# Eighteen chunks of two feed-forward down-projections in seven block products instead of eight

## The reference

```
f = jnp.square(jax.nn.relu(h @ w_ff1[l])) @ w_ff2[l]       # first block: 2048 -> 8192 -> 2048
x = x + gt2 * _rmsnorm(f, g_post_ffn[l])
...
u = jnp.square(jax.nn.relu(h @ w_up[layer]))               # second block, same sizes
x = x + _rmsnorm_2(u @ w_down[layer], norm_mlp_post[layer])
```

## Time and profile before

| | us |
|---|---|
| median of 3 runs | 2550.8 (2550.72 to 2552.91) |
| the profiled execution, its own time | 2552.28 |
| its span, first to last instruction | 2550.5 |
| TensorE matmul busy | 2518.8 (99%) |
| VectorE busy | 1743.5 (68%) |
| ScalarE busy | 1201.3 (47%) |

### The profile page before, as it was taken

One profiled execution on the slowest core, in us unless ns is written; L12 is line 12 of the kernel. 1 busy time (PEld: TensorE's weight loads), 2 busy tenths in 40 slices (PEclk: granted clock), 3 DMA queues, 4 the chain that ended last, 5 costly groups with the idle time before them and its releaser, 6 DMA issues.

```text
span 2550.5 us, 30392 instructions
## 1 busy us (share of the span) xinstructions
PE 2518.8 (99%) x12284; PEld 2102.3 (82%) x12284; DVE 1743.5 (68%) x2351; ACT 1201.3 (47%) x1740; POOL 6.4 (0%) x16
## 2 busy tenths in 40 slices
PE   7999999999999999999999999999999999999998
PEld 4887888888878888888888888888788888888887
DVE  7987988788987866556556565656765574664665
ACT  4444354533456434444344466455554443443443
POOL 0000000000000000000000000000000000000000
PEclk9999999999999999999999999999999999999999
DMA  9984376588876775555555545533545555555553
GB/s 401 415 326 166 123 278 258 196 337 334 340 297 243 283 283 193 199 187 185 200 187 195 207 158 187 192 140 144 200 176 200 182 187 205 185 198 188 183 199 142
DMA packets 78747, 567.12 MB, mean 222 GB/s; under 512 B 8800, under 2 KB 8928, under 8 KB 10256
## 3 DMA queue, kind: packets, MB, share of 16 engines
q1 hardware_dynamic: 77472, 558.09, 59.2%
q0 software_dynamic: 1136, 7.10, 0.7%
HBM read 563.06 MB, written 2.10 MB: 222 GB/s over the span
## 4 chain that ended last, share of the span: by engine, by line
PE 90%; DVE 5%; DMA 2%; ACT 2%; issue 1%; SPq 0%; DVEq 0%; ACTq 0%
PE ps L1238 20%; PE ps L1241 20%; PE ps L1239 20%; PE ps L1296 15%; PE ps L1307 8%; DMA raw<-stream_in 2%; DVE wl L2054 2%; DVE ACC L2088 1%; PE ps L1223 1%; PE ps L1329 1%; PE ps L1578 1%; ACT wh L1645 1%; PE ps L1548 1%; PE ps L1399 0%; PE ps L1333 0%
## 5 line engine op out<-in xcount | busy, mean ns | idle before, releaser
L2054 DVE TENSOR_TENSOR wl<-raw,wh 128x1024 fp32r<-128x1024 f32 x836 | 985.6, 1220 | 538.9 <-ACT wh L1645 537.9
L1645 ACT ACTIVATE wh<-raw 128x1024 fp32r<-128x1024 f32 x836 | 837.4, 1049 | 713.6 <-PE ps L1241 569.8
L1238 PE MATMUL ps<-wh,U 128*128 128x512 f32 x1344 | 525.7, 391 | 0.1
L1241 PE MATMUL ps<-wl,U 128*128 128x512 f32 x1344 | 523.8, 390 | 1.1 <-DVE wl L2054 1.1
L1239 PE MATMUL ps<-wh,U 128*128 128x512 f32 x1344 | 523.0, 389 | 0.0
L1296 PE MATMUL ps<-HT,wh 128*128 128x512 f32 x1792 | 431.7, 391 | 0.0
L1238 PE MATMUL ps<-wh,HT 128*128 128x512 f32 x1080 | 430.0, 398 | 1.0 <-DVE HT L2179 0.9
L1241 PE MATMUL ps<-wl,HT 128*128 128x512 f32 x1080 | 422.0, 391 | 1.5 <-DVE wl L2054 1.5
L1239 PE MATMUL ps<-wh,HT 128*128 128x512 f32 x1080 | 420.8, 390 | 0.0
L1296 PEld LDWEIGHTS ps<-HT,wh 128*128 128x128 f32 x1792 | 328.7, 188 | 63.8 <-issue 0.4
L1241 PEld LDWEIGHTS ps<-wl,U 128*128 128x128 f32 x1344 | 252.3, 188 | 56.4 <-DVE wl L2054 3.5
(11 more groups left out here) (306 smaller groups left out, 1499.8 us busy)
## 6 DMA issues: line engine op xcount, KB each, us to landing
raw<-stream_in SPq DMA_DIRECT2D x524, 1024.0 KB, 4.8
M<-rows_in POOLq DMA_DIRECT2D x6, 1024.0 KB, 5.0
M<-stream_in SPq DMA_DIRECT2D x3, 1024.0 KB, 10.9
y_out<-X SPq DMA_DIRECT2D x3, 512.0 KB, 2.6
X<-x_in SPq DMA_DIRECT2D x1, 1024.0 KB, 5.2
X<-x_in SPq DMA_DIRECT2D x2, 512.0 KB, 14.7
raw<-stream_in SPq DMA_DIRECT2D x1, 640.0 KB, 4.1
raw<-stream_in SPq DMA_DIRECT2D x1, 512.0 KB, 3.3
```

The costliest lines, as they stand in the source:

```text
L1238: e.matmul(o, ah, H[:, c:c + bw], start=k == k0, stop=False)
L1241: ins = e.matmul(o, ah, L[:, c:c + bw], start=False, stop=end)
L1645: e.activation(H, raw[place[n][0]][:, c:c + w], ACT.Copy).then_inc(*hi.tick(p))
L2054: e.tensor_tensor(L, raw[place[n][0]][:, c:c + w], H.bitcast(F32), ALU.subtract).then_inc(*lo.tick(p))
```

## The change

In ten down slabs, 18 chunks (`SEVEN`) are multiplied as 2 by 2 blocks, where rows `t` and steps `k` make the blocks of the hidden matrix, and steps `k` and column blocks `b` those of the weights. Seven block products are formed from sums of blocks. Three products (one from unchanged blocks, one from both, one from a sum) go straight into banks 0, 1 and 2; four go into banks 4 to 7 and are summed over the two such chunks of the slab.

- `blocksums` (VectorE): four sums of 128x512 of the raw weight blocks, into `SUMS` in `M`.
- The chunk is split in four pieces: 1024, 512, 1024 and 1024 columns; the first two come from `raw`, the last two from `SUMS`. They take four places of the ring.
- `combine` (a side task in the second up slab): four operations make the sums of the hidden blocks of both chunks at once, and one copy and one subtraction their halves. For this the hidden tiles of these chunks are kept (`KEPT`).
- `sevenout`: after the last such chunk of a slab one copy by ScalarE and eight operations of 128x512 by VectorE bring banks 4 to 7 into `y`, spread over the next two chunks (one, in the last group's second slab).
- The high half of a tile is an item of its own, `tilehigh`. It stands behind the splits of the next chunk, ahead of `tilelow`.
- `raw` is given back after the second piece's low half.

```diff
+SEVEN = {"fd20": (1, 3), "fd21": (1, 3), "fd30": (1, 3), "fd31": (1,), "gd10": (1, 3), "gd11": (1, 3),
+         "gd20": (1, 3), "gd21": (1, 3), "gd30": (1, 3), "gd31": (1,)}
...
+        if by_seven(name, i) and j == 0:
+            add("blocksums", n)
         add(*only, "split", len(pieces))
+        if by_seven(name, i):
+            pieces.append({"n": n, "ks": None, "width": 512, "w": 512 if j == 1 else 1024, "c": None, "slot": slot,
+                           "before": before, "last": j == 3, "part": j})
+            return
...
             while tiles:
+                add("tilehigh", *tiles[0])
                 add("tilelow", *tiles.popleft())
...
+            elif by_seven(name, i):
+                for p in ps:
+                    add("seven", name, p, i)
+                at["done"] = ps[-1]
                 steps((pace + 1) // 2)
...
+            for q, at_i in enumerate(SEVEN.get(name, ())[-1:] * 4):
+                if i == at_i + (0, 1, 1, 1 if tail else 2)[q]:
+                    add("sevenout", name, q)
...
+            products = {0: [(4, *mine(k, 0)), (0, *mine(k + 1, 0))], 1: [(1, *sums(3))],
+                        2: [(5, *sums(0)), (7, *sums(1))], 3: [(6, *sums(2)), (2, *mine(k + 1, 1))]}[pieces[p]["part"]]
+            for j, (b, ah, al, ready) in enumerate(products):
...
+                e.wait_ge(*hi(p))
+                e.matmul(bank[b][:, :], ah, H[:, c], start=first and b > 3, stop=False)
+                e.matmul(bank[b][:, :], al, H[:, c], start=False, stop=False)
+                e.wait_ge(*lo(p))
+                ins = e.matmul(bank[b][:, :], ah, L[:, c], start=False, stop=last and b > 3)
...
+            if "part" in pieces[p]:
+                if pieces[p]["part"] > 1:
+                    e.wait_ge(*blocksum((n, pieces[p]["part"])))
+                src, H = seven_source(p, H)
+                e.activation(H, src, ACT.Copy).then_inc(*hi.tick(p))
+                return
...
+        def block_sums(n):
+            name, i = events[n][1:]
+            e.wait_ge(*arrived(n))
+            last_use_of_sums(n)
+            e.wait_ge(*combine_l((name[0], int(name[2]))))
+            b = raw[place[n][0]]
+            e.tensor_tensor(SUMS[:, 0:512], b[:, 512:1024], b[:, 0:512], ALU.add).then_inc(*blocksum.tick((n, 0)))
+            e.tensor_tensor(SUMS[:, 512:1024], b[:, 512:1024], b[:, 1536:2048], ALU.add).then_inc(*blocksum.tick((n, 2)))
+            e.wait_ge(*blocksum((n, 0)))
+            e.tensor_tensor(SUMS[:, 1024:1536], SUMS[:, 0:512], b[:, 1536:2048], ALU.add).then_inc(*blocksum.tick((n, 1)))
+            e.wait_ge(*blocksum((n, 1)))
+            e.tensor_tensor(SUMS[:, 1536:2048], SUMS[:, 1024:1536], b[:, 1024:1536], ALU.add).then_inc(*blocksum.tick((n, 3)))
...
+        def combine(task, seg):
...
+            e.tensor_tensor(v[:, 0], z[:, :, 0, 1], z[:, :, 1, 1], ALU.subtract).then_inc(*combine_f.tick((*key, 0)))
+            e.tensor_tensor(v[:, 1], z[:, :, 0, 0], z[:, :, 0, 1], ALU.subtract).then_inc(*combine_f.tick((*key, 1)))
+            e.wait_ge(*combine_f((*key, 0)))
+            e.tensor_tensor(v[:, 2], z[:, :, 0, 0], v[:, 0], ALU.subtract).then_inc(*combine_f.tick((*key, 2)))
+            e.wait_ge(*combine_f((*key, 2)))
+            e.tensor_tensor(v[:, 3], z[:, :, 1, 0], v[:, 2], ALU.subtract).then_inc(*combine_f.tick(key))
```

More of the change, by code:

```diff
@@ L288, in segments @@
     return {"rot": 5, "turnx": 1, "ki": 2, "kr": 2, "index": 21, "mix": 4, "srow": 1, "spread": 1, "gm": 4, "latents": 5,
-            "rest": 5}[kind]
+            "rest": 5, "combine": 2}[kind]
 FIRST_EVAC = {"qA": ("index",), "gb0": ("attention", "B"), "v2": ("attention", "M")}
@@ L351, in split @@
         if n < len(events) and events[n][0] == "g" and n not in parts:
-            for j in range(len(slab_chunks(events[n][1])[events[n][2]])):
+            for j in range(4 if by_seven(*events[n][1:]) else len(slab_chunks(events[n][1])[events[n][2]])):
                 split_piece(n, j, room and room[j])
@@ L448, in run @@
                 tiles.append((name, i))
+                steps((pace + 1) // 2)
+            elif by_seven(name, i):
+                for p in ps:
+                    add("seven", name, p, i)
+                at["done"] = ps[-1]
                 steps((pace + 1) // 2)
@@ L614, in ffn @@
                     later("gm", f, g, s)
+                if s == 0 and seven_chunks(f"{f}d{g}"):
+                    later("combine", f, g)
             for s in range(2):
@@ L982, in beside_halves, with four, seven_source, seven_ks @@
         return v[:, :, 0, :], v[:, :, 1, :], raw[place[n][0]][:, c:c + w].rearrange("p (k n) -> p k n", k=8)
+    def four(n):
+        return raw[place[n][0]][:, 0:2048].rearrange("p (r n) -> p r n", r=4)
+    def seven_source(p, H):
+        part, n = pieces[p]["part"], pieces[p]["n"]
+        if part == 0:
+            return four(n)[:, 0:4:2, :], H.rearrange("p (r n) -> p r n", r=2)
+        if part == 1:
+            return raw[place[n][0]][:, 1536:2048], H
+        return SUMS[:, 1024 * part - 2048:1024 * part - 1024], H
+    def seven_ks(f, g):
+        return [16 * g + 2 * i + j for i in seven_chunks(f"{f}d{g}") for j in range(2)]
+    SUMS, COMBINED = M[:, 0:2048], M[:, 0:1024]
+    COMBINED_H, COMBINED_L = MR[:, 6144:7168], MR[:, 7168:8192]
+    KEPT = M[:, 3072:4096]
+    def combined(v, kind, r):
+        return v[:, 256 * kind + 128 * r:256 * kind + 128 * r + 128]
+    def before_combined(f, g):
+        for s in (1, 0):
+            name = f"{f}d{g - 1}{s}"
+            if name in SEVEN:
+                return gemm(("piece", last_piece[events.index(("g", name, SEVEN[name][-1]))]))
+        return rowed("f") if f == "f" else product(("oa1", 1, 1))
     def stage(name):
@@ L1610, in tensor @@
                 bank_mm(*what)
+            elif kind == "seven":
+                seven_mm(*what)
             elif kind == "thin":
@@ L2007, in scalar @@
                 tile_out(*what)
+            elif kind == "tilehigh":
+                tile_high(*what)
             elif kind == "headsout":
                 heads_out(*what)
+            elif kind == "sevenout":
+                seven_out(*what)
             elif kind == "xsquare":
@@ L2049, in split @@
             e.wait_ge(*hi(p))
+            if "part" in pieces[p]:
+                src, l = seven_source(p, L)
+                _, h = seven_source(p, H)
+                e.tensor_tensor(l, src, h.bitcast(F32), ALU.subtract).then_inc(*lo.tick(p))
+                return
+            if pieces[p]["slot"] == ("M", 0) and "fd31" in SEVEN and events[n][1] == "fd31":
+                e.wait_ge(*extra(("fd31", "y", 0, 1)))
             if events[n][1] == "kr2":
@@ L2555, in vector @@
         tmp[0] = silu, "c"
-        stages = {"split": split, "factor": factor, "diagonal": diagonal_factors, "ada": ada, "colsum": column_sums, "xnorm": x_norm, "evac": evac, "product": product_of,
+        stages = {"split": split, "blocksums": block_sums, "sevenout": seven_out, "factor": factor, "diagonal": diagonal_factors, "ada": ada, "colsum": column_sums, "xnorm": x_norm, "evac": evac, "product": product_of,
                   "total": total, "total2": total_end, "update": update, "norm": norm, "low": low, "xhalves": x_halves, "xfloat": x_float, "xsplit": x_split, "tileout": tile_out,
```

124 lines of the change are left out of this document (115 added, 9 removed).

## The result

The changed kernel takes 2539.28 us, the median of 4 runs (2537.89 to 2541.39). The kernel before, on the same chip and at the same time, takes 2551.56 (2550.72 to 2552.91, 4 runs). The ratio is 0.9949, 95% interval 0.9936 to 0.9961: faster by 12.3 us. The forecast was 2539.2. The profiled execution took 2540.52, its span is 2538.7.

A forecast was written before the change was run, and what follows sets the result against it. It took the number of matmuls on TensorE, 0.2267 us each, as the bound while weight halves arrive in time. 12.2 - 0.1 - 0.45 = 11.7 us saved takes the median from 2550.8 to 2539.2 us, range 2537.8 to 2545.0.

The forecast's parts named there:

- Matmuls, 54 x 0.2267 = 12.2: In 18 down-slab chunks, 3 of 24 matmuls go, each saving its 0.2267 us start distance: 12.2 us.
- the added increments cost nothing: On the seven-product chunks' matmuls, more increments are signalled; each was priced at nothing.
- the pace stays: Remaining matmuls keep starting 0.2267 us apart; the rival, no faster chunks and 2551 us, had a 4% chance.
- Waits in the slabs, 0.1 in gd10, gd20 and gd30: In these first down slabs, the ordinary chunk's low half comes 0.03 us late each, 0.1 in all.
- the spares behind it: Time left before split pieces are due in the down slabs: 0.05 to 1.5 us; rival of thin spares gone, 17%.
- `combine`, 0.15 in three groups, 0.45: In the second block's up slabs, its ScalarE copy makes the following split 0.15 us late, three times: 0.45 us.
- the prediction's sign: What the profile should show: TensorE waits for a high half in gu11, gu21, gu31 at the third tile.
- The lower bound for the sums: `combine`'s four VectorE sums start 0.34 us apart (256 columns), against an upper bound of 0.60 each (512 columns).
- `tilehigh`, "no TensorE wait is there to remove", 0: Moving a tile's high half behind the splits removes ScalarE's wait for the square but gains 0, tiles running at matmul pace.
- one wait list for the whole kernel: In the kernel before, all TensorE waits for a weight's low half were read as 2.6 us together.
- VectorE's busy time: Over the whole kernel, some 153 us are added, taking it from 1743 to about 1897 us.
- 11.7: Total saving over the whole kernel: 12.2 - 0.1 - 0.45 = 11.7 us.

The follow-up runs named there:

- experiment 1: The changed kernel with no chunk in seven products, only the reordering of `tilehigh` kept: 2552.08 us, ratio 0.9994 to the kernel before.
- Experiments 5 and 6: The changed kernel with the first of each seven-product chunk's four block sums made twice: 2541.31 us; with all four made twice: 2571.67 us.
- Experiment 9: The changed kernel with `combine` in three steps, ScalarE's copy one step after VectorE's sums, same 18 chunks: 2539.05 us, ratio 0.9946 to the kernel before.

## Why the prediction was right, and where not

- **Matmuls, 54 x 0.2267 = 12.2:** right. The down slabs' stretches give 12.45 together; 0.3 of it is more than the 9 matmuls of fd30 and fd31: in fd31, a turned tile of `X` (L1457) starts 0.53 after the matmul ahead of it in the kernel before (1476.48, 1477.01), 0.52 in experiment 1, and 0.26 in the changed kernel. That is a wait like the one of the gain between 1587 and 1879 below, and as little explained. That the added increments cost nothing and the pace stays was right too.
- **Waits in the slabs, 0.1 in gd10, gd20 and gd30:** right in size. gd1 and gd2 take 84.38 and 84.39 where 84.32 is the pace, 0.06 each. Experiments 5 and 6 show that the spares behind it were real, smallest in block two.
- **`combine`, 0.15 in three groups, 0.45:** right, 0.13 each, at the third tile of gu11, gu21 and gu31. The four sums of 256 columns (VectorE), the copy and the next split (ScalarE), and TensorE, in the changed kernel's gu11:

```profile
2059.71 0.42 DVE L2239 TENSOR_TENSOR M<-M 128x256 f32<-128x256 f32 x1
...
2060.83 0.42 DVE L2244 TENSOR_TENSOR M<-M 128x256 f32<-128x256 f32 x1
...
2061.29 1.06 ACT L2113 ACTIVATE MR<-M 128x1024 fp32r<-128x1024 f32 x1 [2.88 <-DVE M L2244]
2062.25 1.99 ACT L1761 ACTIVATE wh<-raw 128x1024 fp32r<-128x1024 f32 x2
...
2061.55 3.94 PE L1404 MATMUL ps<-HT,wh 128*128 128x512 f32 x16
2065.34 2.08 PE L1415 MATMUL ps<-HT,wl 128*128 128x256 f32 x16
```

  A row of 16 high steps takes 3.66 us to the next row elsewhere, 3.79 here: two starts, 2063.44 and 2063.75, come 0.27 and 0.31 after the ones ahead, when the copy of 2062.25 has delivered its first half. The wait list names none of this, against the prediction's sign; it shows in the starts alone. The lower bound for the sums was the right end. Experiment 9 took this wait away.
- **`tilehigh`, "no TensorE wait is there to remove", 0: this step failed.** It gains 1.5 us in fd00, and holds off 1.8 in gd10, gd20 and gd30. The prediction took one wait list for the whole kernel, 2.6 us for all low halves, as too small to ask where they stand. Two of these nine were at fd00's first chunk, and their cause was the very wait of ScalarE that `tilehigh` moves. And the list's 0.6 us stands for 1.5 in the starts.
- **A gain of 0.7 between 1587 and 1879** was not forecast. TensorE waits there for a turned tile of `X`, once: 0.7 before, 1.3 in experiment 1, not at all with the seven products. ScalarE had waited 3.2 (before), 3.8 (experiment 1) and 2.5 (changed) for a load just ahead. Why that load lands sooner is open.
- **VectorE's busy time** was given as 1897 and is 1873. The additions were priced at 0.685 each and last that; taken one by one, the durations in the trace add up to 151 us more than before (153 were worked out), and 22 of that overlap in the queue and count once. ScalarE likewise: 41 more singly, 27 as busy time. It had no part in the sum.
- **The number.** By its own steps the change was worth 11.7, by the stretches it is worth 14.3. That the forecast met the measured time was luck: in the profiled execution (2540.6 forecast, 2540.52 measured) the 2.6 us of unforecast gain were offset by an untouched stretch 2.4 us longer than before, and for the median the forecast started from 2550.8, the median of three runs, where longer sets gave 2551.6 to 2552.9. Of the sum, the 12.2 and the 0.45 are shown; the agreement to 0.1 us is not.

## What to carry to other kernels

When TensorE runs at its matmuls' pace, price a removed matmul by the distance of starts, and spend the work on the queue that delivers its operands: take each deadline by itself, for an average of 75% busy hid both a spare of 0.05 us and a loss of 34. Ask of every short wait in the list where it stands before a reordering is priced at nothing, since an in-order engine that waits for one result holds back all copies behind it. Compare stretches between fixed events, not only spans, when an untouched stretch moves by more than what is asked about.

## What was not expected of the hardware

The untouched stretch took from 387.9 to 392.3 us in twelve profiled executions of kernels that don't differ in it. TensorE's waits for low halves in it come to 0.5 us in the shortest of the changed kernel's three (388.29), 1.6 in its longest (390.94) and 1.8 in experiment 9 (392.25), and they stand at places that change. One of them, in the changed kernel's first profile (ScalarE, VectorE, TensorE):

```profile
735.69 2.01 ACT L1761 ACTIVATE wh<-raw 128x1024 fp32r<-128x1024 f32 x2 [4.74 <-DMA raw<-stream_in]
...
736.79 2.36 DVE L2202 TENSOR_TENSOR wl<-raw,wh 128x1024 fp32r<-128x1024 f32 x2 [0.93 <-ACT wh L1761]
...
738.07 0.50 PE L1312 MATMUL ps<-wl,HT 128*128 128x512 f32 x1 [0.53 <-DVE wl L2202]
```

A load lands late, and the chain copy, subtraction, matmul follows; in the other two executions of that kernel this matmul starts in time. But ScalarE's waits for weights in the stretch do not go with its length: 111.3 us in 37 waits before (388.54), 116.7 in 37 in the changed kernel (390.94), 109.3 in 35 in experiment 9, the longest. So some of the length is late loads, and what makes them late, or the rest, is not settled. In the rest of the kernel, stretches of 85 to 135 us repeated within 0.1 us from run to run and from chip to chip, kernel by kernel.
